# Layer norms whose sums lie in PSUM banks on VectorE and shift by the first tile; modulation tiles moved between up-projections

## The chip, the cores and the metric

The kernel runs on one core of one Trainium2 chip. A core has TensorE (PE in the profile; PEld is its weight load), VectorE (DVE), ScalarE (ACT), GpSimd (POOL) and SyncE (SP), each with its own queue of instructions, run in order. They tell each other of finished work through semaphores. SBUF and PSUM have 128 partitions; PSUM has eight banks of 512 fp32 columns. TensorE writes to PSUM alone, and GpSimd can't reach PSUM. The metric is the device time of one execution in microseconds (us).

## The reference

Four blocks follow each other on 512 tokens of width 1024 (blocks 2 and 3 also see 256 context tokens). Each block has a mixer (mLSTM, differential attention, convolution with a Fourier transform, neighbourhood attention) and a feed-forward part. Blocks 0 and 1 are built so:

```python
for i in range(2):
    ada = silu(c) @ w_ada[i] + b_ada[i]
    sh1, sc1, g1, sh2, sc2, g2 = split(ada, 6)
    u = x * (1 + sc1) + sh1
    y = mixer_i(u)
    x = layer_norm(ALPHA * x + (1 + g1) * y, ln_g[i, 0], ln_b[i, 0])
    u = x * (1 + sc2) + sh2
    h = causal_dwconv3(u @ w_up[i])            # 2 * 2816 channels
    a, g = split(h, 2)
    y = (gelu(g) * a) @ w_down[i]
    x = layer_norm(ALPHA * x + (1 + g2) * y, ln_g[i, 1], ln_b[i, 1])
```

Blocks 2 and 3 use RMS norms and a squared ReLU, with modulation vectors from `c_2` and `c_ctx_2`. All is fp32.

## The kernel before

**Layout.** Everything is feature-major: `XT` holds the residual stream as eight tiles of 128 features x 512 tokens. fp32 products are made of three matmuls with operands split into a high part (fp32r) and a low part: (WH, xh), (WH, xl), (WL, xh). A weight job is one output tile: SyncE loads 128 x 1024 fp32 into one of two `RAW` buffers (`load_raw`, L457), ScalarE rounds it into `WH` (`round_hi`, L788, or L857 in loops), GpSimd makes the low part `WL` (`lo`, L549), and TensorE runs 24 matmuls (L1503; L1177 in the value projection of block 1). `WH` and `WL` have four slots. `load_raw(j)` waits until the low part of job j-2 is made, and TensorE's job j waits for its own low part. Jobs are numbered through; the phases that matter here are the mixer's output projection `res`, and then for the feed-forward part three groups of an up-projection `up` (16, 16, 12 jobs) and a down-projection `down` (8 jobs each, the last with 18 matmuls a job). In block 0, `res` is jobs 32 to 39, the first `up` 40 to 55; in block 1 they are 132 to 139 and 140 to 155.

**Modulation.** The products with `w_ada` run on VectorE. SyncE loads a tile of 128 x 1024 (`load_ada`, L463, issued behind a weight load of the same queue), and VectorE multiplies it with the broadcast condition and sums (`ada_job`, L1630; two products, L1626 and L1627, for the tiles 96 to 159). A phase with `ada=a` does one tile per job, ahead of the job's own epilogue, from tile a on; `ada_out` writes four results into `MOD`. There are 192 tiles. The first up-projections carry 16 each, the third ones none.

**Up-projection epilogue.** ScalarE makes the first tap (L966), VectorE the two others out of the bank (`conv`, L1706), ScalarE the GELU, VectorE the product (`ffn_prod`, L638), ScalarE the high part (L634), VectorE the low part `Hl` (`ffn_lo`, L642). TensorE's down-projection waits for `Hl` tile by tile.

**Layer norms.** There are four, numbered by `idx` = 0 to 3, behind `res` and behind the last `down` of blocks 0 and 1. The variance is taken of shifted values. In the phase's first four jobs VectorE sums the finished tiles of `XT` into `ZS` (`sum_x`, L1714). TensorE multiplies the sum by 1/1024 into bank 5 (L1508), VectorE takes twice this mean of half the features off each tile (`shift`, L1729) and adds tiles 4 to 7 to `ZS` (L1734). ScalarE squares the tiles into `SQ` (L928). GpSimd adds squares 0 to 6 (`sum_squares`, L538), between the low parts of the next phase's first jobs. `ln_pe` sums over features with MEAN, token by token:

```python
pe.wait_ge(S("sq_add"), 6 * idx + 6)
token_sums(BANK[6], 0, SQ[:, 0], True, False)
pe.wait_ge(S("z_sum"), 2 * idx + 2)
token_sums(BANK[1], 0, ZS[:, 0:T], True, True).then_inc(S("d_sum"), 1)
pe.wait_ge(S("squared"), 8 * idx + 8)
token_sums(BANK[6], 0, SQ[:, 7], False, True).then_inc(S("var_sum"), 1)
```

A matmul with MEAN follows (L1542). `ln` on VectorE then centres (L1931) and scales (L1941) the tiles. ScalarE makes `U1h` and `UF`, and VectorE `U1l`. GpSimd's `norm_pool` (L511) applies gain and bias to `XT` as each `UF` tile is done, between its low parts of jobs 2 and 3 of the next phase. TensorE's first two jobs of that phase run side by side, tile by tile of `U1h` and `U1l`.

Of the kernel before, what the change touches and what calls it, by code (L numbers as in the profile page):

```python
# [54 lines left out]
LN_TILES = (((4, 0), (5, 1, 2), (6, 3), (7,)),) * 2 + (((), (4, 5, 0), (6, 1, 2, 3), (7,)), ((4, 0), (5, 1, 2), (6, 3), (7,)))  # L55
LN_HALF = (0, 0, 1, 0)

LN_MEAN = (3, 3, 3, 0)

NV_NORMS = ((0,), (1, 2), (3,), (4,), (5,), (6,), (7,), ())  # L60


def plan():
# [3 lines left out]
    def add(kind, n, layer, src, fill, nk=KT, ctx=False, ada=None, **more):  # L67
        nonlocal j0
        phases.append(dict(kind=kind, n=n, layer=layer, src=src, fill=fill, nk=nk, ctx=ctx, ada=ada,
                           j0=j0, seen=kinds.get(kind, 0), **more))  # L70
        j0 += n
        kinds[kind] = kinds.get(kind, 0) + n
        if ada is not None:
            assert ada == adas[-1]
            adas.append(ada + n)
# [16 lines left out]
    h = ffn(0, 8, 0, (40, 56, 64, 80, None, None))  # L92
# [4 lines left out]
    h = ffn(1, 24, h, (96, 112, 120, 136, None, None))  # L97
# [102 lines left out]
def build(nc, a, out):  # L200
    with ExitStack() as stack:
# [186 lines left out]

        def peeled(p):

            return p["j0"] == 0 or (p["seen"] == 0 and p["kind"] in ("v", "up", "na_k", "na_v", "res"))
# [59 lines left out]
        def _(sp):  # L451
# [28 lines left out]
            for n, p in enumerate(phases):  # L480
                def body(i, p=p, ada_before=None):
                    for u in range(4):
# [8 lines left out]
                if p["n"] > 4:  # L491
                    with sp.Fori(1, p["n"] // 4) as i:
                        body(i)
                pending = p["ada"] + p["n"] - 4 if p["ada"] is not None else None
# [8 lines left out]
        def norm_pool(pool, p):  # L503
            idx = 2 * p["layer"] + (p["kind"] == "down")
            for t in range(KT):
# [3 lines left out]
                else:  # L509
                    pool.wait_ge(S("uf_done"), 8 * UFILL[idx] + t + 1)  # L510
# [34 lines left out]
        def _(pool):  # L545
# [51 lines left out]
            for n, p in enumerate(phases):  # L597
# [23 lines left out]
                lo(p["j0"] + 3, 3, 1)  # L621
                if p["n"] > 4:
# [158 lines left out]
        def _(act):  # L781
# [138 lines left out]
            def shifted_squares(idx, u):  # L920

                if idx == 3 and u == 0:
# [3 lines left out]
                for n, t in ln_slots(idx, u):  # L926
# [3 lines left out]
            def epilogue(i, p, u):  # L930

                bank_out(i, p, u)
                if ends_in_ln(p) is not None and not is_first(i):
                    shifted_squares(ends_in_ln(p), u)
# [472 lines left out]
        def _(pe):  # L1407
# [72 lines left out]
            def stream(i, p):  # L1480
# [3 lines left out]
                for u in range(2 if after_norm else 0, 4):  # L1484
# [50 lines left out]
            def ln_pe(idx):  # L1535
                pe.wait_ge(S("sq_add"), 6 * idx + 6)
                token_sums(BANK[6], 0, SQ[:, 0], True, False)
# [3 lines left out]
                token_sums(BANK[6], 0, SQ[:, 7], False, True).then_inc(S("var_sum"), 1)  # L1541
                pe.matmul(BANK[LN_MEAN[idx]][:], MEAN[:], ZS[:, 0:T], start=True, stop=True).then_inc(S("mean_sum"), 1)  # L1542
# [67 lines left out]
        def _(dve):  # L1610
# [105 lines left out]
            def shift(i, p, u):  # L1716

                idx = ends_in_ln(p)
                if is_first(i):
                    sum_x(u)  # L1720
                    if u == 3:
                        dve.sem_inc(S("z_sum"), 1)
                    return
                if u == LN_HALF[idx]:
                    dve.wait_ge(S("mean_sum"), 2 * idx + 1)
                    link(dve.scalar_tensor_tensor(out=ZS[:, 0:T], in0=BANK[5][:], scalar=-8.0, in1=ZS[:, 0:T],
                                                  op0=ALU.mult, op1=ALU.add))
                for n, t in ln_slots(idx, u):
                    dve.scalar_tensor_tensor(out=XT[:, t], in0=BANK[5][:], scalar=-2.0, in1=XT[:, t], op0=ALU.mult, op1=ALU.add)\  # L1729
                        .then_inc(S("shifted"), 1)  # L1730
                for n, t in ln_slots(idx, u):
                    if t >= 4:
                        dve.wait_ge(S("shifted"), 8 * idx + n + 1)
                        link(dve.tensor_tensor(ZS[:, 0:T], ZS[:, 0:T], XT[:, t], ALU.add))  # L1734
# [179 lines left out]
            def ln(p, idx, nxt):  # L1914
# [12 lines left out]
                link(dve.tensor_tensor(SM[:, 48:52], BANK[6][:, 0:4], SM[:, 44:48], ALU.subtract))  # L1927
                dve.tensor_scalar(SM[:, 48:52], SM[:, 48:52], 0.0, None, ALU.max).then_inc(S("var_ready"), 1)

                def centre(t):  # L1930
                    dve.tensor_tensor(XT[:, t], XT[:, t], BANK[LN_MEAN[idx]][:], ALU.subtract).then_inc(S("centred"), 1)  # L1931
# [252 lines left out]
            for n, p in enumerate(phases):  # L2184
# [26 lines left out]
                def body(i, p=p):  # L2211
                    for u in range(4):
                        if p["ada"] is not None:
                            ada_job(i, p["ada"], u)
                        epilogue(i, p, u)
                    if p["ada"] is not None:
# [181 lines left out]
```

## Time and profile before

| | |
|---|---|
| median of 3 runs | 2957.94 us (2956.37 to 2958.21) |
| the profiled execution's own time | 2959.11 us |
| its span, from the first to the last instruction | 2957.3 us |
| mean granted TensorE clock | 0.972 |
| busy: PE, PEld | 2800.1 us (95%), 2392.5 us (81%) |
| busy: DVE, ACT, POOL | 1606.1 (54%), 1046.6 (35%), 1134.4 (38%) |
| chain that ended last, by engine | PE 81%, DVE 10%, issue 3%, POOL 3% |

Busy time is the union of an engine's instructions in the profile. The chain is followed back from the last instruction, at each step to what released it. A row of the timeline gives start, duration, engine (a q marks the queue's own work, such as issuing a DMA), line, operation, what it writes and reads, form, count, and in brackets the engine's idle time just before it with what ended it. The granted clock is given as a share of the upper of TensorE's two levels, 2.4 GHz; 0.50 is the lower one, 1.2 GHz. Matmuls are pipelined, so that a row's duration is longer than the distance to the next start.

### The profile page before, as it was taken

The page shows a single profiled execution, that of the slowest core. Times are in us where ns is not written, and L with a number is a line of the kernel's source. Part 1 is how long each engine was busy: PE and PEld are TensorE (multiplying, and loading weights), DVE is VectorE, ACT ScalarE, POOL GpSimd, SP SyncE. Part 2 cuts the span into 40 slices and gives each one's busy share as a digit, 9 for nine tenths or more (in the row PEclk, how much of TensorE's full clock was granted, in tenths as well). Part 3 has the DMA queues.
Part 4 walks back from the last instruction along what each step waited for, and adds up shares of the span by engine and source line. Part 5 has one row for each costly group of instructions (what it writes and reads, how often), then busy time and mean ns, then how long its engine had stood idle before and what let it go on. Part 6 is the DMA issues. An engine that isn't in the chain of part 4 may idle for free.

```text
span 2957.3 us, 38329 instructions
## 1 busy us (share of the span) xinstructions
PE 2800.1 (95%) x13904; PEld 2392.5 (81%) x13904; DVE 1606.1 (54%) x2329; ACT 1046.6 (35%) x1689; POOL 1134.4 (38%) x534
## 2 busy tenths in 40 slices
PE   4998899999999798999899999999999999999998
PEld 3885687887776687887897999999997977778887
DVE  6536885946455787976622332755453386432111
ACT  3333443423465443424321231212223337433222
POOL 2440554445522454445521243323235233334443
PEclk9998899999899899999799999999999999999999
DMA  5351355542421145543121122333332122122232
GB/s 214 109 185 43 114 195 188 185 149 93 144 83 61 57 176 181 197 149 114 45 64 59 56 74 76 138 119 129 127 128 78 53 95 65 61 82 97 93 99 85
DMA packets 89956, 329.84 MB, mean 112 GB/s; under 512 B 9956, under 2 KB 10724, under 8 KB 89320
## 3 DMA queue, kind: packets, MB, share of 16 engines
q1 hardware_dynamic: 85392, 312.21, 30.3%
q10 hardware_dynamic: 4440, 16.00, 1.6%
q8 instruction: 75, 1.23, 0.2%
q14 instruction: 49, 0.40, 0.0%
HBM read 324.50 MB, written 2.10 MB: 110 GB/s over the span
## 4 chain that ended last, share of the span: by engine, by line
PE 81%; DVE 10%; issue 3%; POOL 3%; ACT 2%; DMA 1%; DVEq 0%; ACTq 0%; SPq 0%; POOLq 0%
PE pair L1501 26%; PE pair L1503 26%; PE bank L1503 12%; PE pair L1192 3%; PE pair L1343 1%; DVE ADA L1630 1%; PE bank L1296 1%; PE pair L1359 1%; PE bank L1376 1%; DMA ADA<-in_ast 1%; DVE Hl L642 1%; DVE TA L638 1%; PE pair L1177 1%; PE bank L1177 1%; PE bank L1218 1%
## 5 line engine op out<-in xcount | busy, mean ns | idle before, releaser
L549 POOL TENSOR_TENSOR WL<-RAW,WH 128x1024 fp32r<-128x1024 f32 x392 | 977.4, 2495 | 1611.4 <-ACT WH L857 1089.3
L857 ACT ACTIVATE WH<-RAW 128x1024 fp32r<-128x1024 f32 x276 | 290.3, 1052 | 343.9 <-PE pair L1501 181.5
L1630 DVE CUSTOM_DVE_ANT_0 ADA<-ADA,CB 128x1024 f32<-128x1024 f32 x128 | 222.2, 1741 | 113.6 <-DMA ADA<-in_ast 102.5
L1750 DVE SCALAR_TENSOR_TENSOR XT<-pair,GATE,XT 128x512 f32 (+1 forms) x96 | 72.0, 751 | 346.4 <-PE pair L1503 180.5
L1501 PE MATMUL pair<-Uh,WH 128*128 128x384 f32 x832 | 214.1, 338 | 2.1 <-issue 1.6
L1501 PE MATMUL pair<-Uh,WL 128*128 128x384 f32 x832 | 211.1, 334 | 0.0
L1501 PE MATMUL pair<-Ul,WH 128*128 128x384 f32 x832 | 211.1, 334 | 0.0
L1503 PE MATMUL pair<-Hh,WH 128*128 128x512 f32 x432 | 173.2, 401 | 19.1 <-DVE Hl L642 19.1
L1503 PE MATMUL bank<-U1h,WH 128*128 128x512 f32 x480 | 187.3, 390 | 0.0
L1503 PE MATMUL bank<-U1h,WL 128*128 128x512 f32 x480 | 186.8, 389 | 0.0
L1503 PE MATMUL bank<-U1l,WH 128*128 128x512 f32 x480 | 186.7, 389 | 0.0
L1503 PE MATMUL pair<-U1h,WH 128*128 128x512 f32 x448 | 174.7, 390 | 0.0
L1503 PE MATMUL pair<-U1h,WL 128*128 128x512 f32 x448 | 174.4, 389 | 0.0
L1503 PE MATMUL pair<-U1l,WH 128*128 128x512 f32 x448 | 174.3, 389 | 0.0
L1503 PE MATMUL pair<-Hl,WH 128*128 128x512 f32 x432 | 171.0, 396 | 0.0
L1503 PE MATMUL pair<-Hh,WL 128*128 128x512 f32 x432 | 170.9, 396 | 0.0
L788 ACT ACTIVATE WH<-RAW 128x1024 fp32r<-128x1024 f32 x116 | 122.2, 1054 | 116.6 <-DMA RAW<-in_wst 54.4
L1501 PEld LDWEIGHTS pair<-Uh,WH 128*128 128x128 f32 x832 | 150.2, 188 | 6.1 <-issue 5.3
L1806 DVE SCALAR_TENSOR_TENSOR TT<-pair,TT 128x512 f32<-128x512 f32 x64 | 44.3, 692 | 197.3 <-ACT TT L978 103.5
L1501 PEld LDWEIGHTS pair<-Ul,WH 128*128 128x128 f32 x832 | 150.2, 188 | 0.0
L1501 PEld LDWEIGHTS pair<-Uh,WL 128*128 128x128 f32 x832 | 150.2, 188 | 0.0
L1501 PE MATMUL pair<-Hl,WH 128*128 128x384 f32 x512 | 129.9, 334 | 0.0
(408 smaller groups left out, 6244.6 us busy)
## 6 DMA issues: line engine op xcount, KB each, us to landing
RAW<-in_wst SPq DMA_DIRECT2D x392, 512.0 KB, 3.5
ADA<-in_ast SPq DMA_DIRECT2D x192, 512.0 KB, 4.5
NB<-in_nbias ACTq DMA_DIRECT2D x8, 768.0 KB, 4.2
XT<-in_xt SPq DMA_DIRECT2D x1, 2048.0 KB, 15.5
STRIP<-in_strip ACTq DMA_DIRECT2D x8, 256.0 KB, 2.8
CB<-in_cb ACTq DMA_DIRECT2D x4, 512.0 KB, 4.0
DX<-in_dx ACTq DMA_DIRECT2D x1, 2048.0 KB, 7.9
out_xt<-XT SPq DMA_DIRECT2D x1, 2048.0 KB, 6.2
```

The lines of the kernel that those rows point to most:

```text
L549: pool.tensor_tensor(WL[:, s4], RAW[:, s2], WH[:, s4].bitcast(F32), ALU.subtract)\
L638: dve.tensor_tensor(TA2[:, half], TA2[:, half], TG[:, half], ALU.mult).then_inc(S("ffn_prod"), 1)
L642: dve.tensor_tensor(flat(Hl[:, ds(tile, 1), 0:T]), TA2[:, half], flat(Hh[:, ds(tile, 1), 0:T]).bitcast(F32), ALU.subtract).then_inc(S("h_r ...
L788: act.activation(WH[:, u], RAW[:, u % 2], ACT.Copy).then_inc(S("hi_done"), 1)
L857: act.activation(WH[:, c % 4], RAW[:, c % 2], ACT.Copy).then_inc(S("hi_done"), 1)
L1177: mm = pe.matmul(BANK[VT_BANKS[half][b]][:], x[:, k, b * P:(b + 1) * P], flat(w[:, i, 4 * kk:4 * kk + 4]), start=k == 0 and m == 0, stop=k ...
L1192: mm = pe.matmul(BANK[j % 2][:], w[:, j % 4, k], x[:, k], start=k == 0 and m == 0, stop=k == KT - 1 and m == 2)
L1501: mm = pe.matmul(dst, w[:, u, k], x[:, k, c:c + HALF_TC], start=st and m == 0, stop=en and m == 2)
L1503: mm = pe.matmul(bank_of(p, u)[:], w[:, u, k], x[:, k, 0:T], start=st and m == 0, stop=en and m == 2)
L1630: dve.tensor_tensor_reduce(tile, tile, cb[:, 0], 1.0, 0.0, ALU.mult, ALU.add, AD[:, u, 0:1])\
L1750: ins = dve.scalar_tensor_tensor(out=flat(XT[:, ds(jl, 1)]), in0=bank[:], scalar=gate_of(jl), in1=flat(XT[:, ds(jl, 1)]), op0=ALU.mult, op ...
L1806: ins = dve.scalar_tensor_tensor(out=TT[:, u % 2, 0:T], in0=bank[:], scalar=0.0, in1=TT[:, u % 2, 0:T], op0=ALU.max, op1=ALU.mult)
```

## The change

**Sums and shift.** The shift is now eight times the feature mean of `XT[:, 0]` (`LN_SHIFT` names the job behind which TensorE makes it: 1, or 4 for norm 2). `LN_TILES` now gives for each of the eight jobs the tiles that are shifted in it. VectorE adds the shifted tiles in a PSUM bank (the last add writes `ZS`), and it also adds the squares 0 to 5 in another bank (`add_squares`; the last add writes `SQ[:, 0]`), a job later. Squares 6 and 7 are summed by TensorE as they are. GpSimd's `sum_squares` is gone. `LN_BANKS` names the banks. ScalarE loads the table of the square root in job 6 of the phase for norms 1 to 3.

**norm_pool.** For norms 0 to 2 it moves behind the low part of job 3 and waits for all eight `U1l` tiles instead of `UF` tile by tile.

**Modulation tiles.** The first up-projection of blocks 0 and 1 has them in its second half only (8 of 16 jobs). The phases after it carry on from there, and the last eight tiles are in the first eight of the third up-projection's 12 jobs. SyncE's and VectorE's loops of these four phases are written out.

```diff
-LN_TILES = (((4, 0), (5, 1, 2), (6, 3), (7,)),) * 2 + (((), (4, 5, 0), (6, 1, 2, 3), (7,)), ((4, 0), (5, 1, 2), (6, 3), (7,)))
-LN_HALF = (0, 0, 1, 0)
-
-LN_MEAN = (3, 3, 3, 0)
+LN_SHIFT = (1, 1, 4, 1)
+LN_TILES = (((), (0, 1), (2,), (3,), (4,), (5,), (6,), (7,)),) * 2 + \
+           (((), (), (), (), (0, 4, 1), (5, 2), (6, 3), (7,)), ((), (0, 1), (2,), (3,), (4,), (5,), (6,), (7,)))
+
+LN_BANKS = ((6, 3, 2, 3), (6, 3, 2, 3), (6, 7, 4, 3), (6, 3, 2, 0))
...
+ADA_GROUPS = {40: (2, 4), 80: (0, 2), 96: (2, 4), 136: (0, 2)}
...
-    h = ffn(0, 8, 0, (40, 56, 64, 80, None, None))
+    h = ffn(0, 8, 0, (40, 48, 56, 72, 80, None))
...
-    h = ffn(1, 24, h, (96, 112, 120, 136, None, None))
+    h = ffn(1, 24, h, (96, 104, 112, 128, 136, None))
...
+        def brings_ada(p, i):
+
+            return p["ada"] is not None and (p["ada"] not in ADA_GROUPS or p["groups"][0] <= i < p["groups"][1])
...
-                        elif not is_first(i) and p["ada"] is not None:
-                            load_ada(i * 4 + (p["ada"] - 4 + u), u % 2)
+                        elif not is_first(i) and brings_ada(p, i - 1):
+                            load_ada(i * 4 + (p["ada"] - 4 - 4 * p["groups"][0] + u), u % 2)
...
-                    pool.wait_ge(S("uf_done"), 8 * UFILL[idx] + t + 1)
+                    pool.wait_ge(S("u_ready"), 8 * UFILL[idx] + KT)
...
-        def sum_squares(pool, idx, n):
-
-            if n == 1:
-                pool.wait_ge(S("squared"), 8 * idx + 1)
-            else:
-                pool.wait_ge(S("sq_add"), 6 * idx + n - 1)
-            pool.wait_ge(S("squared"), 8 * idx + n + 1)
-            pool.tensor_tensor(SQ[:, 0], SQ[:, 0], SQ[:, n], ALU.add).then_inc(S("sq_add"), 1)
...
-                idx = ends_in_ln(before) if before is not None else None
                 for u in range(3):
                     lo(p["j0"] + u, u, u % 2)
-                    if idx is not None and u < 2:
-                        for n in ((1, 2, 3, 4), (5, 6))[u]:
-                            sum_squares(pool, idx, n)
-                if idx is not None:
+                idx = ends_in_ln(before) if before is not None else None
+                if idx == 3:
                     norm_pool(pool, before)
...
                 lo(p["j0"] + 3, 3, 1)
+                if idx is not None and idx != 3:
+                    norm_pool(pool, before)
...
+                if idx >= 1 and (i, u) == (1, 2):
+                    act.preload_act_table_set("sqrt_and_others")
...
-                    if idx is not None and not is_first(i) and u == LN_HALF[idx]:
+                    if idx is not None and 4 * i + u == LN_SHIFT[idx]:
                         pe.wait_ge(S("z_sum"), 2 * idx + 1)
-                        pe.matmul(BANK[5][:], MEAN[:], ZS[:, 0:T], start=True, stop=True).then_inc(S("mean_sum"), 1)
+                        pe.matmul(BANK[5][:], MEAN[:], XT[:, 0], start=True, stop=True).then_inc(S("mean_sum"), 1)
...
             def ln_pe(idx):
-                pe.wait_ge(S("sq_add"), 6 * idx + 6)
-                token_sums(BANK[6], 0, SQ[:, 0], True, False)
+                by_token, rest = (BANK[b] for b in LN_BANKS[idx][2:])
+                pe.wait_ge(S("sq_add"), 5 * idx + 5)
+                token_sums(by_token, 0, SQ[:, 0], True, False)
+                pe.wait_ge(S("squared"), 8 * idx + 7)
+                token_sums(by_token, 0, SQ[:, 6], False, False)
...
+                idx, jl = ends_in_ln(p), 4 * i + u
+                shifted, squares = (BANK[b] for b in LN_BANKS[idx][:2])
+                if jl == 0:
+                    dve.sem_inc(S("z_sum"), 1)
+                if jl == LN_SHIFT[idx]:
+                    dve.wait_ge(S("mean_sum"), 2 * idx + 1)
+                for n, t in ln_slots(idx, jl):
+                    dve.scalar_tensor_tensor(out=XT[:, t], in0=BANK[5][:], scalar=-8.0, in1=XT[:, t], op0=ALU.mult, op1=ALU.add)\
+                        .then_inc(S("shifted"), 1)
+                for n, t in ln_slots(idx, jl):
+                    dve.wait_ge(S("shifted"), 8 * idx + n + 1)
+                    if n:
+                        first_tile = XT[:, LN_TILES[idx][LN_SHIFT[idx]][0]]
+                        link(dve.tensor_tensor(ZS[:, 0:T] if n == 7 else shifted[:], first_tile if n == 1 else shifted[:], XT[:, t],
+                                               ALU.add))
+                if jl > LN_SHIFT[idx]:
+                    for n, t in ln_slots(idx, jl - 1):
+                        if not (idx == 2 and n == 5):
+                            add_squares(idx, n, squares)
+                if idx == 2 and jl == 6:
+                    add_squares(idx, 5, squares)
+
+            def add_squares(idx, n, squares):
+
+                if n == 0 or n > 5:
                     return
...
+                dve.wait_ge(S("squared"), 8 * idx + n + 1)
+                dve.tensor_tensor(SQ[:, 0] if n == 5 else squares[:], SQ[:, 0] if n == 1 else squares[:], SQ[:, n], ALU.add)\
+                    .then_inc(S("sq_add"), 1)
+                dve.wait_ge(S("sq_add"), 5 * idx + n)
...
-                        if p["ada"] is not None:
-                            ada_job(i, p["ada"], u)
+                        if brings_ada(p, i):
+                            ada_job(i - p["groups"][0], p["ada"], u)
...
-                if ends_in_ln(p) is not None:
-                    body(0)
-                    body(1)
+                if ends_in_ln(p) is not None or p["ada"] in ADA_GROUPS:
+                    for i in range(p["n"] // 4):
+                        body(i)
```

## Rows read from the trace of the kernel before

**Rows 1.** Who waited for whom (us in total, times, longest us), TensorE, whole span.
```profile
PE bank L1516 <- POOL SQ L538: 23.1, 4, 8.6
PE pair L1503 <- DVE Hl L642: 19.1, 11, 8.8
```

**Rows 2.** Timeline, the exit of norm 0.
```profile
340.93 0.43 SPq L463 DMA_DIRECT2D ADA<-in_ast  x1
...
345.76 1.23 DVE L1630 CUSTOM_DVE_ANT_0 ADA<-ADA,CB 128x1024 f32<-128x1024 f32 x1 [4.69 <-DMA ADA<-in_ast]
...
348.36 0.69 DVE L1734 TENSOR_TENSOR ZS<-ZS,XT 128x512 f32<-128x512 f32 x1
...
349.17 1.87 PE L1516 MATMUL pair<-MEAN,ZS 128*128 128x1 f32 x8 [3.71 <-DVEq L1916]
```

**Rows 3.** Timeline, the exit of norm 1.
```profile
734.63 1.23 DVE L1734 TENSOR_TENSOR ZS<-ZS,XT 128x512 f32<-128x512 f32 x1
...
740.12 1.85 PE L1516 MATMUL pair<-MEAN,ZS 128*128 128x1 f32 x8
```

**Rows 4.** The instructions of L1931 (duration ns min/median/max).
```profile
L1931 DVE TENSOR_TENSOR XT<-XT,pair x32: 673/680/689, 354.7 to 1424.6; 128x512 f32<-128x512 f32 x32
```

**Rows 5.** Timeline, the exit of norm 3.
```profile
1406.91 1.22 DVE L1734 TENSOR_TENSOR ZS<-ZS,XT 128x512 f32<-128x512 f32 x1
1408.28 3.67 DVE L1924 TENSOR_REDUCE CSQ<-UF 128x256 f32<-128x2048 f32 x1 [0.15 <-DVE ZS L1734]
...
1412.38 1.84 PE L1516 MATMUL pair<-MEAN,ZS 128*128 128x1 f32 x8
```

**Rows 6.** Timeline, the exit of norm 2.
```profile
1001.75 1.66 DVE L1740 SCALAR_TENSOR_TENSOR XT<-XT,TT 128x512 f32<-128x512 f32 x1
...
1015.32 1.84 PE L1516 MATMUL pair<-MEAN,ZS 128*128 128x1 f32 x8
```

**Rows 7.** Timeline of VectorE, job 1 of block 0's first up-projection.
```profile
380.15 3.44 DVE L1630 CUSTOM_DVE_ANT_0 ADA<-ADA,CB 128x1024 f32<-128x1024 f32 x1 [6.02 <-DMA ADA<-in_ast]
```

**Rows 8.** Waits of TensorE at 447-461, 585-592, 1112-1132 and 1255-1266.
```profile
PE pair L1503 <- DVE Hl L642: 3.4, 2, 2.2
...
PE pair L1503 <- DVE Hl L642: 0.9, 1, 0.9
...
PE pair L1503 <- DVE Hl L642: 9.3, 2, 8.8
...
PE pair L1503 <- DVE Hl L642: 1.7, 2, 1.2
```

**Rows 9.** Windows: length, busy us of PE, PEld, DVE, ACT, POOL, clock, DMA, GB/s.
```profile
372.00:448.00 76.00, 76.00 (x337) 62.90 (x337) 67.27 (x75) 33.70 (x44) 36.73 (x16) 1.00 0.56 201
...
457.00:461.00 4.00, 4.00 (x10) 3.07 (x10) 3.84 (x3) 1.64 (x2) 2.76 (x2) 0.50 0.14 47
...
1127.00:1132.00 5.00, 4.00 (x9) 2.70 (x10) 3.74 (x6) 2.54 (x4) 2.10 (x1) 0.50 0.02 5
```

**Rows 10.** Timeline: ScalarE's high part of job 3, TensorE's start of job 4, three phases.
```profile
370.31 1.05 ACT L788 ACTIVATE WH<-RAW 128x1024 fp32r<-128x1024 f32 x1
...
382.72 0.39 PE L1503 MATMUL pair<-U1h,WH 128*128 128x512 f32 x1
...
761.23 1.05 ACT L788 ACTIVATE WH<-RAW 128x1024 fp32r<-128x1024 f32 x1
...
775.29 0.39 PE L1177 MATMUL bank<-WH,U1h 128*128 128x512 f32 x1
...
1039.75 1.04 ACT L788 ACTIVATE WH<-RAW 128x1024 fp32r<-128x1024 f32 x1
...
1049.11 0.39 PE L1503 MATMUL pair<-U1h,WH 128*128 128x512 f32 x1
```

**Rows 11.** The instructions of L511 (duration ns min/median/max).
```profile
L511 POOL TENSOR_SCALAR XT<-XT,PRM x32: 772/1273/2327, 359.4 to 1430.1; 128x512 f32<-128x512 f32 x32
```

**Rows 12.** Groups of VectorE's instructions, 1037.8 to 1114.4 (busy us, mean ns, idle before).
```profile
L1706 DVE SCALAR_TENSOR_TENSOR TA<-pair,PRM,TA 128x511 f32<-128x511 f32 (+1 forms) x8 | 6.0, 747 | 0.5 <-DVE TA L1706 0.5
```

More of the change, by code:

```diff
@@ L68, in add @@
         nonlocal j0
-        phases.append(dict(kind=kind, n=n, layer=layer, src=src, fill=fill, nk=nk, ctx=ctx, ada=ada,
+        groups = ADA_GROUPS.get(ada, (0, n // 4))
+        phases.append(dict(kind=kind, n=n, layer=layer, src=src, fill=fill, nk=nk, ctx=ctx, ada=ada, groups=groups,
                            j0=j0, seen=kinds.get(kind, 0), **more))
@@ L74, in add @@
             assert ada == adas[-1]
-            adas.append(ada + n)
+            adas.append(ada + 4 * (groups[1] - groups[0]))
     add("qk", 16, 0, "u", 0)
@@ L487, in body @@
                             load_ada(ada_before + u, u % 2)
-                        elif not is_first(i) and p["ada"] is not None:
-                            load_ada(i * 4 + (p["ada"] - 4 + u), u % 2)
+                        elif not is_first(i) and brings_ada(p, i - 1):
+                            load_ada(i * 4 + (p["ada"] - 4 - 4 * p["groups"][0] + u), u % 2)
                 body(0, ada_before=pending)
-                if p["n"] > 4:
+                if p["ada"] in ADA_GROUPS:
+                    for i in range(1, p["n"] // 4):
+                        body(i)
+                elif p["n"] > 4:
                     with sp.Fori(1, p["n"] // 4) as i:
                         body(i)
-                pending = p["ada"] + p["n"] - 4 if p["ada"] is not None else None
+                pending = p["ada"] + 4 * (p["groups"][1] - p["groups"][0]) - 4 if brings_ada(p, p["n"] // 4 - 1) else None
             if pending is not None:
@@ L918, in rms_act, with shifted_squares @@
                     context_hi(KT - 1)
-            def shifted_squares(idx, u):
-                if idx == 3 and u == 0:
+            def shifted_squares(idx, i, u):
+                if idx >= 1 and (i, u) == (1, 2):
+                    act.preload_act_table_set("sqrt_and_others")
+                if idx == 3 and (i, u) == (1, 0):
                     act.wait_ge(S("ct_land"), 16)
@@ L925, in shifted_squares @@
                         act.activation(UF[:, t, T:TC], CT[:, t], ACT.Square).then_inc(S("ctx_sq"), 1)
-                for n, t in ln_slots(idx, u):
+                for n, t in ln_slots(idx, 4 * i + u):
                     act.wait_ge(S("shifted"), 8 * idx + n + 1)
@@ L932, in epilogue @@
                 bank_out(i, p, u)
-                if ends_in_ln(p) is not None and not is_first(i):
-                    shifted_squares(ends_in_ln(p), u)
+                if ends_in_ln(p) is not None:
+                    shifted_squares(ends_in_ln(p), i, u)
             def bank_out(i, p, u):
@@ L1540, in ln_pe @@
                 pe.wait_ge(S("squared"), 8 * idx + 8)
-                token_sums(BANK[6], 0, SQ[:, 7], False, True).then_inc(S("var_sum"), 1)
-                pe.matmul(BANK[LN_MEAN[idx]][:], MEAN[:], ZS[:, 0:T], start=True, stop=True).then_inc(S("mean_sum"), 1)
+                token_sums(by_token, 0, SQ[:, 7], False, True).then_inc(S("var_sum"), 1)
+                pe.matmul(rest[:], MEAN[:], ZS[:, 0:T], start=True, stop=True).then_inc(S("mean_sum"), 1)
                 if idx == 3:
@@ L1716, in shift @@
             def shift(i, p, u):
[L1718 to L1722, printed above, removed]
-                    return
[L1724 to L1734, printed above, removed]
+                idx, jl = ends_in_ln(p), 4 * i + u
```

10 lines of the change are left out of this document (6 added, 4 removed).

## Prediction, made before the change was run

> **What bounds the kernel now.** I read the page first: TensorE has work nearly throughout (the table above), so time can only be won where it stands or runs on a lower clock. The list of who waited for whom, cut to TensorE, names those places [rows 1]. Two of the groups lie where the change works. Four waits of 23.1 us together are for the sums of squares on GpSimd, one behind each layer norm. Eleven waits of 19.1 us together are for the low part of a hidden tile (`Hl`, L642), where a down-projection starts. I then read the timeline of each place. I call the norms N0 to N3 by `idx`, and give stretches in the profile's time.
>
> **The exits of the norms.** In the old code the last token sum over `ZS` may start only behind VectorE's last `ZS` add and behind the sum over `SQ[:, 0]`, which waits for GpSimd. What follows it (the sum over `SQ[:, 7]`, the mean matmul, centring) is the same in both kernels, so the start of the `ZS` sum measures each exit.
>
> N0: it starts at 349.17 [rows 2]. The last step's VectorE work is late because the modulation tile lands only at 345.7: it was issued at 340.93, behind a weight load that waits for GpSimd's low part, and that stood behind three sums of squares. Without those, low part 41 ends some 5 us earlier (about 335.7), its weight load and the modulation tile are issued at about 336.3, and the tile lands at about 341.0 by the same 4.7 us. Then come the tile product 1.2 (with up to 1 us of a lock), the residual 0.7, the shift 0.7 and the add 0.7: 345.3. Gain 3.9, with 3.0 and 5.5 as ends.
>
> N1: the last add starts at 734.63 and takes 1.23 because GpSimd runs; in a bank it takes the 0.68 of an operation that reads a bank and `XT` [rows 3, 4]. So 735.4 instead of 740.12: gain 4.7 (4.2 to 4.8). N3 is alike: 1406.91 + 0.68 and the hop give 1407.7 instead of 1412.38, gain 4.7 (4.0 to 4.8) [rows 5]. Here the context's `TENSOR_REDUCE` of 3.67 now starts at 1407.7 and ends at 1411.4, just when the last squares' sum does (1407.7 + 3.6). It costs nothing, but it would be what is late next.
>
> N2: VectorE has more to do, because shifts start only at job 4. From 1001.75 [rows 6] the step of tile 6 is residual 0.7, two shifts 1.4, two adds 1.3, three adds of squares 2.0 and a wait of 0.5 for ScalarE: 1007.7. The last tile needs 2.1 more: 1009.7 instead of 1015.32. Gain 5.6 (3 to 7).
>
> Together 18.9. VectorE's added work is three operations of 0.68 for each norm (20 instead of 17) and hides in the jobs: a step without a modulation tile is 2.8 us against jobs of 4.1 (18 matmuls of 0.226).
>
> The Trainium skill speaks against this ("VectorE: DVE Perf Modes", section "The TRN2 errata"): an operation that reads PSUM pays 120 fixed cycles where one from SBUF pays 58. By that page each exit would lose an estimated 0.065 us, 0.26 in all. The trace doesn't agree: 0.68 us with one operand in a bank [rows 4], 0.69 with both in SBUF at 348.36 [rows 2].
>
> **The first half of the first up-projection.** VectorE starts it late: at 380.15 it has waited 6.0 us for a modulation tile, whose product then takes 3.44, against 1.23 at 345.76 [rows 2, 7]. In block 1, where a tile costs two such products, it hardly catches up. The bill comes at the end of the phase, as `Hl` is late: 3.4 us of TensorE's wait in block 0 and 9.3 in block 1, where the second up-projections, also with a tile in each job but no norm ahead, pay 0.9 and 1.7 [rows 8]. Without tiles in the first eight jobs VectorE is freed of at least 8 x 1.2 us in block 0 and 16 x 1.2 in block 1, more than the lag. So the first up-projections should end like the second ones: 2.5 and 7.6 gained. Behind the longer waits TensorE's clock falls to the lower of its two levels (0.50 of the upper): from 457 to 461 it ran 10 matmuls, and in block 1 9 in 4.0 busy us, where 17.7 fit at the 0.226 us each of the phase's 76 us [rows 9]. That is 1.7 and 2.0 lost, and the slow clock lasts a little beyond both windows: I take 2.0 and 2.9. Together 4.5 + 10.5 = 15.0 (from 10.5, if block 0 ends no better than its third up-projection and block 1 keeps some lag, to 15.5).
>
> The eight tiles go to the third up-projection, jobs 0 to 7 of 12. Their DMAs go through SyncE's queue in the same pattern as in the second, where no weight came late. Four jobs without tiles follow, so its end stays. Cost 0; were that cover missing, up to the 10.5 of block 1. The loops written out in full I cost at 0.
>
> **norm_pool behind the low part of job 3.** This is the term against. The eight gain operations (L511) used to run between `U1l` tiles, mostly hidden. Now they stand between the low parts of jobs 3 and 4. ScalarE frees the high part of job 3 at the same point as before, so GpSimd ends low part 3 at about 373.8, 764.7 and 1043.3 (1.05 and 2.40 behind the starts of L788 at 370.31, 761.23 and 1039.75). TensorE wants low part 4 at 382.72, 775.29 and 1049.11 [rows 10]. In between must fit 8 d + 2.4, where d is the mean of L511: least 0.77, median 1.27, longest 2.33 [rows 11]. At 0.77 the stalls are 0, 0 and 2.8. At the median they are 3.7, 2.0 and 6.8: 12.5. I take 0.92: VectorE's operations there mostly read a bank (L1706, 0.747 on average with GpSimd at work [rows 12]), and only two `TA`/`Hl` operations can collide, 0.6 each. That gives 0.9, 0 and 4.0. The clock lost 2.0 behind a wait of 3.4, so I add that to the last: 6.9 in all. The ends are 2.8 and 19 (the median, with 2.0, 2.0 and 2.9 of clock). Queued behind it is also a weight load on SyncE, which waits for low part 4. It is due two jobs later (10.9 us), and landing 3.5, high part 1 and low part 2.4 fit.
>
> The Trainium skill has a rule for this ("SBUF — State Buffer", section "Who interferes with whom"): VectorE contends with GpSimd when both of its inputs are in SBUF, and the loser waits for the whole operation; with one input there is no contention. The trace agrees with the second half by the 0.747 of L1706. By that rule the stalls are the 4.9 us I took, by the median the 12.5.
>
> **Sum.** 18.9 + 15.0 - 6.9 = 27.0. The profiled execution took 2959.1 (its span is 2957.3); less 27.0 is 2932.1. The median of the runs shown is 2957.9, 1.2 lower, so I predict 2931.
>
> **Rivals.**
> 1. *As forecast*, 62%: 2931, own range 2925 to 2938.
> 2. *GpSimd's gain operations keep their old median*, 16%: 19 instead of 6.9, so 2943. For it: that is what they took. Against: then `U1l`, with both inputs in SBUF, ran beside them.
> 3. *Slower: the moved norm_pool starves TensorE*, 5%. At the longest duration, 2.33, the stalls are 12.1, 10.4 and 15.2 = 37.7, and each is followed by a slow clock as behind the 8.8 us wait, 2.9 each: 46.4, more than the 33.9 gained, so 2970. It decides from d = 1.8 (24 d - 18.1 + 8.7 = 33.9). Against it: only modulation products keep GpSimd off so long, and these have left that half.
> 4. *The tiles take their stall along* to the third up-projection, 7%: up to 10.5 back, 2941. For it: in block 1 a tile costs VectorE two products in each job. Against: four free jobs behind.
> 5. *The lag isn't from the tiles* but from the norm, so the ends of the first up-projections stay (the change does not do what it says), 6%: 15 less, 2946. Against: the 6.0 wait is for a tile.
> 6. Other, 4%.
>
> Cases 1, 2, 4 and most of 5 lie between 2923 and 2946, which leaves out the slower case and tails of the first, some 15 to 20%. A measurement of this kernel tells about 0.2% (6 us) from no change. Faster by more: 91%. Within: 4%. Slower: 5%.
>
> **What would show it.** No `SQ` on GpSimd, and TensorE's `ZS` sums some 4 to 5.6 us sooner behind the last job of each norm's phase. The waits for L642 at the first down-projections near 1 and 2 us. VectorE without a modulation product in the first eight jobs. L511 in one block behind low part 3 at 0.77 to 1 us each, and TensorE waiting for GpSimd's low part at job 4 of block 1, some 4 us. I am wrong if that wait is above 8, if waits for `Hl` come up in the third down-projection, or if the `ZS` sums move by under 3 us.

## The result, and the profile after

The changed kernel takes 2936.45 us (median of 4 runs, 2934.43 to 2938.15), the kernel before, on the same chip, 2958.07: ratio 0.9926, 95% interval 0.9913 to 0.9938. That is 21.6 us less, where 27 were forecast; 2931 was predicted, and 2936.45 lies within the range of 2923 to 2946. The profiled execution took 2937.88 us, with a span of 2936.1 against 2957.3. TensorE is busy for 2797.1 us, VectorE 1593.2, GpSimd 1093.2.

The waits of TensorE over the whole span, after (answers to [rows 1]; columns: us in total, times, longest):

```profile
PE pair L1507 <- DVE Hl L644: 8.1, 10, 1.2
...
PE bank L1520 <- DVE SQ L1752: 5.1, 1, 5.1
...
PE pair L1520 <- DVE SQ L1752: 4.3, 1, 4.3
```

The wait for hidden tiles fell from 19.1 to 8.1 us, and none is longer than 1.2. The 23.1 us for GpSimd's sums are gone. But two waits for sums of squares have come up on VectorE, 4.3 us in norm 0 and 5.1 in norm 2.

To find where time came from, I took the starts of TensorE's first and last matmul of each phase in both traces and set them against the terms of the prediction:

| stretch | before, us | after, us | gain | predicted |
|---|---|---|---|---|
| norm 0: last matmul of `res` to first of `up` | 19.35 | 20.04 | -0.7 | 3.9 |
| block 0, first up and down | 139.19 | 133.36 | 5.8 | 4.5 - 0.9 |
| block 0, third down | 37.41 | 35.57 | 1.8 | 0 |
| norm 1 | 18.63 | 13.55 | 5.1 | 4.7 |
| block 1, value projection, to the first scores | 61.19 | 64.90 | -3.7 | 0 |
| norm 2 | 20.28 | 18.47 | 1.8 | 5.6 |
| block 1, first up | 89.32 | 93.58 | -4.3 | -6.0 |
| block 1, first down | 56.29 | 45.50 | 10.8 | 10.5 |
| norm 3 | 32.12 | 27.37 | 4.7 | 4.7 |

These make 21.3 us; the span lost 21.2. The row of the value projection runs on through two and a half jobs of the next projection, up to the first matmul of the attention scores; all of its 3.7 us were lost in the value projection itself. Norms 1 and 3 and the down-projections came out near what was worked out, and the first up-projection of block 1 lost less. Norms 0 and 2 gave 1.1 of the 9.5 us predicted for them, and the value projection lost 3.7 that weren't foreseen.

**Norm 0.** Timeline after, one turn of what sets its pace and the end (answers to [rows 2]):

```profile
337.05 0.63 ACT L932 ACTIVATE SQ<-XT 128x512 f32<-128x512 f32 x1 [4.35 <-DVE XT L1732]
337.59 1.04 ACT L790 ACTIVATE WH<-RAW 128x1024 fp32r<-128x1024 f32 x1
...
338.71 2.39 POOL L552 TENSOR_TENSOR WL<-RAW,WH 128x1024 fp32r<-128x1024 f32 x1 [4.11 <-ACT WH L790]
...
341.13 0.33 SPq L467 DMA_DIRECT2D RAW<-in_wst  x1
341.50 0.43 SPq L473 DMA_DIRECT2D ADA<-in_ast  x1
...
346.14 2.49 DVE L1637 CUSTOM_DVE_ANT_0 ADA<-ADA,CB 128x1024 f32<-128x1024 f32 x1 [1.16 <-DMA ADA<-in_ast]
...
348.56 0.68 DVE L1760 SCALAR_TENSOR_TENSOR XT<-XT,TT 128x512 f32<-128x512 f32 x1
349.28 0.69 DVE L1732 SCALAR_TENSOR_TENSOR XT<-bank,XT 128x512 f32<-128x512 f32 x1
350.00 0.69 DVE L1738 TENSOR_TENSOR ZS<-bank,XT 128x512 f32<-128x512 f32 x1
350.00 0.63 ACT L932 ACTIVATE SQ<-XT 128x512 f32<-128x512 f32 x1 [4.30 <-DVE XT L1732]
```

Read it from square to square. ScalarE's square at 337.05 had waited 4.35 us for VectorE's shift; the high part queued behind it, then GpSimd's low part, the weight load, the modulation tile behind that on SyncE (341.50; 340.93 before), its product on VectorE, residual, shift, and the square at 350.00. That is 12.95 us for two jobs of 5.44. The work goes around a ring: each part waits for the one before it, and the last one feeds the first again, two jobs later, at 6.5 us a job. The product of 2.49 is part of it, 1.23 without a wait: it started beside a low part (345.20 to 347.55). Without those 1.26 us a turn would be 5.85 us a job, an estimate from these rows, still more than 5.44. In the kernel before, ScalarE did that high part 6.1 us ahead of the phase's last matmul (339.42), here 2.8 us ahead (340.38), and GpSimd's sums delayed only the low part behind it:

```profile
332.39 5.34 POOL L538 TENSOR_TENSOR SQ<-SQ 128x512 f32<-128x512 f32 x3 [0.38 <-ACT SQ L928]
...
333.35 1.04 ACT L788 ACTIVATE WH<-RAW 128x1024 fp32r<-128x1024 f32 x1
...
337.69 2.83 POOL L549 TENSOR_TENSOR WL<-RAW,WH 128x1024 fp32r<-128x1024 f32 x1
```

**Norms 1 and 3.** The `ZS` sums, after (answers to [rows 3] and [rows 5]): 2.8 us behind each phase's last matmul, 7.5 before. Before, the last add had ended at 735.86 in norm 1, and TensorE waited for GpSimd's sums up to 740.12; that wait was 4.3 us. The context's reduction of 3.63 starts right behind the add and ends 0.2 us behind the last squares' sum, as foreseen.

```profile
729.39 1.46 PE L1520 MATMUL pair<-MEAN,ZS 128*128 128x1 f32 x8 [0.75 <-DVEq L1936]
...
1391.93 1.78 PE L1520 MATMUL pair<-MEAN,ZS 128*128 128x1 f32 x8 [0.75 <-DVEq L1936]
1391.98 3.63 DVE L1944 TENSOR_REDUCE CSQ<-UF 128x256 f32<-128x2048 f32 x1 [0.16 <-DVE ZS L1738]
```

**Norm 2.** Timeline after (answers to [rows 6]):

```profile
988.66 0.67 ACT L992 ACTIVATE TT<-pair,GATE 128x512 f32<-128x512 f32 x1
988.84 2.39 POOL L552 TENSOR_TENSOR WL<-RAW,WH 128x1024 fp32r<-128x1024 f32 x1 [4.16 <-ACT WH L790]
989.43 2.34 DVE L1760 SCALAR_TENSOR_TENSOR XT<-XT,TT 128x512 f32<-128x512 f32 x1 [0.95 <-ACT TT L992]
...
1002.13 0.69 DVE L1752 TENSOR_TENSOR SQ<-bank,SQ 128x512 f32<-128x512 f32 x1
1002.86 1.02 DVE L1760 SCALAR_TENSOR_TENSOR XT<-XT,TT 128x512 f32<-128x512 f32 x1
...
1002.88 3.54 PE L1520 MATMUL bank<-MEAN,SQ 128*128 128x1 f32 x16 [5.11 <-DVE SQ L1752]
1006.28 1.84 PE L1520 MATMUL pair<-MEAN,ZS 128*128 128x1 f32 x8
```

The residual (`XT` and `TT`, both in SBUF) takes 2.34 us where 0.7 was put in: GpSimd's low part began 0.59 us ahead of it, and it ended 0.5 us behind that low part. The `ZS` sum starts 8.9 us behind the phase's last matmul (997.38), 10.7 before, 5.1 predicted. VectorE's last add had ended at 1005.32; the sum stood 0.9 us longer behind the 16 matmuls over the squares, which waited for the add at 1002.13.

**norm_pool.** GpSimd's eight gain operations, and TensorE at job 4 of block 1's up-projection:

```profile
754.12 6.06 POOL L524 TENSOR_SCALAR XT<-XT,PRM 128x512 f32<-128x512 f32 x8
...
1034.04 6.06 POOL L524 TENSOR_SCALAR XT<-XT,PRM 128x512 f32<-128x512 f32 x8
...
1042.65 0.47 PE L1507 MATMUL pair<-U1h,WH 128*128 128x512 f32 x1 [2.79 <-POOL WL L552]
```

They take 0.76 us each, where 0.92 was taken; the stall of 2.8 is what was worked out for 0.77. In the 5 us behind it the granted clock is 0.66. The windows from 1043 to 1048 and of the rest of the phase (columns as in [rows 9]):

```profile
1043.00:1048.00 5.00, 5.00 (x17) 3.91 (x16) 2.60 (x2) 2.05 (x3) 2.68 (x2) 0.66 0.61 210
...
1048.00:1109.00 61.00, 61.00 (x271) 50.51 (x270) 48.00 (x65) 26.06 (x35) 31.78 (x13) 1.00 0.48 172
```

The value projection, jobs 4 to 6 of GpSimd and SyncE:

```profile
760.14 4.75 POOL L552 TENSOR_TENSOR WL<-RAW,WH 128x1024 fp32r<-128x1024 f32 x2
762.57 0.33 SPq L467 DMA_DIRECT2D RAW<-in_wst  x1
...
766.03 1.06 ACT L790 ACTIVATE WH<-RAW 128x1024 fp32r<-128x1024 f32 x1 [6.14 <-DMA RAW<-in_wst]
766.99 1.07 ACT L963 ACTIVATE VD<-pair 128x512 f32<-128x512 f32 x2
...
767.62 0.80 PE L1181 MATMUL pair<-WH,U1h 128*128 128x512 f32 x1 [2.52 <-ACT VD L963]
```

TensorE doesn't wait for a low part here. It waits for ScalarE's copies out of its banks, which stand behind a high part, whose weight load waited for low part 4, which waited for norm_pool.

### The profile page after: what moved, and what is told of

The parts are those of the page before. It is cut to its first block, busy times and chain, and to the rows that moved or that the text cites. A ratio compares the mean times of both kernels' runs of the same rounds, so it can differ in the third digit from the quotient of the medians.

```text
span 2936.1 us, 37960 instructions
## 1 busy us (share of the span) xinstructions
PE 2797.1 (95%) x13936; PEld 2391.5 (81%) x13936; DVE 1593.2 (54%) x2341; ACT 1046.6 (36%) x1689; POOL 1093.2 (37%) x510
## 3 DMA queue, kind: packets, MB, share of 16 engines
q8 instruction: 75, 1.23, 0.2%
## 4 chain that ended last, share of the span: by engine, by line
PE 58%; DVE 2%; POOL 1%; ACT 1%; issue 1%; DVEq 0%; ACTq 0%; POOLq 0%
PE pair L1505 26%; PE pair L1507 18%; PE bank L1507 4%; PE pair L1347 1%; PE bank L1300 1%; PE pair L1363 1%; PE bank L1380 1%; PE bank L1347 1%; PE bank L1437 0%; PE pair L1461 0%; PE pair L1320 0%; PE bank L1320 0%; POOL UF L534 0%; PE bank L1287 0%; POOL UF L538 0%
## 5 line engine op out<-in xcount | busy, mean ns | idle before, releaser
L1637 DVE CUSTOM_DVE_ANT_0 ADA<-ADA,CB 128x1024 f32<-128x1024 f32 x128 | 237.7, 1863 | 117.2 <-DMA ADA<-in_ast 105.9
L1505 PE MATMUL pair<-Hh,WL 128*128 128x384 f32 x512 | 129.9, 334 | 0.0
```

Of the source, the lines that this page charges most:

```text
L1505: mm = pe.matmul(dst, w[:, u, k], x[:, k, c:c + HALF_TC], start=st and m == 0, stop=en and m == 2)
L1637: dve.tensor_tensor_reduce(tile, tile, cb[:, 0], 1.0, 0.0, ALU.mult, ALU.add, AD[:, u, 0:1])\
```

## The experiments

Each kernel was timed beside the kernel before (2958.7 to 2959.8 us in these runs). Intervals are 95%. A norm's time is counted from TensorE's last matmul of the projection to its first of the next phase, as in the table.

**tiles_only.** The kernel before with the modulation tiles' part of the diff alone (`ADA_GROUPS`, the list of the phases' tiles, the loops written out).

> The kernel before with the modulation tiles moved and nothing else; the norms and norm_pool are the old ones. Theory 1 (the parts add up): in the changed kernel's trace the first up- and down-projections gained 5.8 us in block 0 and 10.8 in the down-projection of block 1, and the last up-projections of block 0 1.8 more; all of it comes from the tiles, so this kernel gains 16 to 18.5 of the 21.6 us: 2940 to 2942, with waits of about 1 us for the low part of the hidden tile at both first down-projections. Theory 2 (part of the lag came from the old norms, whose last additions start VectorE late into the up-projection): it gains under 13, above 2945, and a wait of over 3 us for the hidden tile stays in one of the blocks.

Measured: 2945.74 us (2945.26 to 2948.99, 5 runs), ratio 0.9958 [0.9944, 0.9971]: 12.9 gained. Both first down-projections wait 1.2 us at most at a time; block 0's first down takes 44.27 us, its third 35.61, block 1's first down 45.47: 18.3 gained there, as theory 1 has it. But 5.8 us are lost in block 1's attention, where nothing was edited. Its trace there:

```profile
875.97 2.34 POOL L558 TENSOR_TENSOR WL<-RAW,WH 128x1024 fp32r<-128x1024 f32 x1 [7.18 <-ACT WH L797]
876.00 2.72 DVE L2102 SCALAR_TENSOR_TENSOR PD<-ZD,SM,PD 128x384 f32<-128x384 f32 x1
...
878.78 0.90 PE L1237 MATMUL bank<-IDENT,PD 128*128 128x128 f32 x3 [2.27 <-DVE PD L2102]
```
```profile
870.00:885.00 15.00, 12.48 (x51) 9.07 (x49) 9.27 (x24) 6.32 (x21) 2.34 (x1) 0.77 0.20 69
```

VectorE's operation began 0.03 us behind GpSimd's low part and took 2.72 us; in the changed kernel the same one (876.42, 0.62 us) missed it. TensorE waited 2.3, and over these 15 us its clock was 0.77, against 1.00 before. So neither theory's total fits: the tiles gave all of the 18.3, and an accident of phase took 5.8 back. That it is an accident is argued, not shown: it was not tried by itself. No other kernel here shows it.

**tiles_unmoved.** The other half: the changed kernel with `ADA_GROUPS = {}` and the old list of tiles.

> The changed kernel with the modulation tiles where they were: only the norms and norm_pool's place are changed. Theory 1 (the parts are not independent: norm_pool's eight gain operations now meet a modulation product of VectorE in each job, and each such product or gain operation waits for the other): the 18.3 us of the tiles are lost, and the gain operations take 1.2 us or more each instead of 0.76, so that TensorE waits some 4 us more in each of the three phases: 2958 to 2968, no faster than the kernel before. Theory 2 (the parts add up, gain operations stay at 0.76): 2936.5 + 18.3 = 2954.8.

Measured: 2962.46 us (2958.03 to 2967.46, 11 runs), ratio 1.0012 [1.0003, 1.0021]: slightly slower than before. (The profiled execution took 2967.45, the second longest of the eleven.) GpSimd's eight gain operations now take 7.02 us in block 0 and 9.03 in block 1, and TensorE waits twice as long at job 4 there:

```profile
1048.55 9.03 POOL L524 TENSOR_SCALAR XT<-XT,PRM 128x512 f32<-128x512 f32 x8
```
```profile
PE pair L1507 <- POOL WL L552: 5.7, 1, 5.7
```

The first down-projections lose more than the tiles had cost: 52.53 and 55.03 us, 17.8 more than in the changed kernel, where moving the tiles had gained 16.5. The parts depend on each other, as in theory 1, though its 1.2 us for each gain operation was too much (0.88 and 1.13).

**pool_old_place.** norm_pool back, the rest as changed:

```diff
-                    pool.wait_ge(S("u_ready"), 8 * UFILL[idx] + KT)
+                    pool.wait_ge(S("uf_done"), 8 * UFILL[idx] + t + 1)
-                if idx == 3:
+                if idx is not None:
                     norm_pool(pool, before)
                 lo(p["j0"] + 3, 3, 1)
-                if idx is not None and idx != 3:
-                    norm_pool(pool, before)
```

> The changed kernel with norm_pool for norms 0 to 2 back between the low parts of jobs 2 and 3, tile by tile behind UF. Theory 1 (the move costs what TensorE's segments lost: 3.7 us in block 1's value projection, 4.3 in its first up-projection): 8 us faster than the changed kernel, about 2928.5, and no wait of TensorE for the low part of a weight near 765 us, none of 3 us at job 4 of the up-projection. Theory 2 (GpSimd's gain operations only shift which low part is late; in the old place low part 3 is, and more of them meet operations of VectorE with two operands in SBUF): 2934 to 2938, with waits at job 3. Theory 3: the 3.7 us in the value projection come from the new sums around norm 1 and not from norm_pool, so only about 4 come back: 2932.

Measured: 2929.31 us (2925.86 to 2930.95), ratio 0.9897 [0.9882, 0.9912], 7.1 below the changed kernel. The value projection takes 60.86 us and block 1's first up 89.59: 4.0 each, theory 1. A gain operation's median there is 1.27 us again, and costs nothing: it stands in work that waits for ScalarE anyway. Its trace also has norm 1 at 11.66 us against 13.55, and the next kernel's at 11.39, where nothing was edited: in the 3 us behind the `ZS` sum the granted clock was 0.90 here (731 to 734) and 0.58 in the changed kernel (729.4 to 732.4). A difference of 2 us in one stretch can be the clock alone.

**vt_copies_first.** In the value projection's fourth job:

```diff
                     for u in range(4):
-                        round_next(i, p, u)
+                        late = p["kind"] == "vt" and is_first(i) and u == 3
+                        if not late:
+                            round_next(i, p, u)
                         epilogue(i, p, u)
+                        if late:
+                            round_next(i, p, u)
```

> The changed kernel with one thing swapped: in the fourth job of block 1's value projection ScalarE copies the four banks out (VD) first and only then makes the high part of the weight three jobs on. Theory 1 (TensorE's wait of 2.52 us at 767.62 is for those copies, which stand behind a high part whose weight load is late: it waits for low part 4, that for norm_pool): the wait goes, block 1's value projection takes about 61.5 instead of 64.90 us, and the time is 3 to 3.5 less, about 2933. Theory 2 (behind the copies TensorE would wait for the low parts themselves, which are as late): the wait moves to the low part of weight 5 or 6 and less than 1 us comes back, 2936.

Measured: 2932.81 us (2929.98 to 2936.83), ratio 0.9916 [0.9902, 0.9929]; the value projection 61.09. Copies at 762.56, no wait behind them, though norm_pool is still where the change put it: theory 1.

```profile
762.56 1.09 ACT L963 ACTIVATE VD<-pair 128x512 f32<-128x512 f32 x2 [5.44 <-PE bank L1185]
```

**squares_later.** ScalarE squares the tiles of a job behind the next high part:

```diff
+                if ends_in_ln(p) is not None and 4 * i + u > 0:
+                    shifted_squares(ends_in_ln(p), *divmod(4 * i + u - 1, 4))
                 bank_out(i, p, u)
-                if ends_in_ln(p) is not None:
+                if ends_in_ln(p) is not None and (i, u) == (1, 3):
                     shifted_squares(ends_in_ln(p), i, u)
```

> The changed kernel with ScalarE's square of each shifted tile one job later, behind the high part of the next weight instead of ahead of it. Theory 1 (norm 0 is late through a ring: the square waits for VectorE's shift and holds up the high part, that the low part, the weight load, the modulation tile behind it in SyncE's queue, and that VectorE's next step; 6.5 us a turn against 5.44 us of a job): the modulation products of the last steps start at TensorE's pace, TensorE's sum over ZS in norm 0 starts 3 to 5 us sooner, the other norms change by less than 1, and the time is 2931.5 to 2933.5. Theory 2 (norm 0 is late because VectorE and GpSimd lock each other out in each step, which the order on ScalarE doesn't touch): the sum over ZS moves by less than 1 us and the time stays at 2935.5 to 2937.5.

Measured: 2931.41 us (2929.69 to 2933.06), ratio 0.9905 [0.9889, 0.992]. Norm 0 fell from 20.04 to 12.67 us: the ring was open, the last tile was issued at 334.62 and the `ZS` sum stands 3.4 us behind the last matmul (340.57), where the changed kernel had 10.4.

```profile
334.62 0.43 SPq L473 DMA_DIRECT2D ADA<-in_ast  x1
...
339.41 1.35 DVE L1639 CUSTOM_DVE_ANT_0 ADA<-ADA,CB 128x1024 f32<-128x1024 f32 x1 [0.26 <-DMA ADA<-in_ast]
...
343.98 1.52 PE L1522 MATMUL pair<-MEAN,ZS 128*128 128x1 f32 x8 [1.35 <-DVEq L1938]
```

With the order went also most of the wait in the product, 1.35 instead of 2.49 us; how much of the 7.4 us is the order alone and how much that wait was not taken apart. The other norms changed little, but norm 2 lost 1.1 (19.56).

**both** and **two_edits.** Both edits; then the same with norm 2 keeping its order (`later = idx in (0, 1, 3)`).

> Both edits together: norm_pool in its old place and ScalarE's squares one job later. Theory 1 of both: the gains add, as they lie in other stretches (norm 0's phase; the jobs behind norms 1 and 2): 2936.5 - 8 - 4 = 2924.5. If only the order on ScalarE matters, 2932; if only norm_pool's place, 2928.5.

> norm_pool in its old place, and ScalarE's squares one job later for norms 0, 1 and 3 alone; norm 2 keeps its order. Theory 1 (with the later squares norm 2 took 19.55 us from the last matmul of its projection to the first of the up-projection, against 18.47 with the early ones, since the order on ScalarE isn't what holds it): norm 2 is back at 18.5 and the time is 1 us below the kernel with both edits, 2923.5. Theory 2 (the 1.1 us are chance): 2924.5 as there.

Measured: 2924.74 us (2923.98 to 2926.0), ratio 0.9883 [0.9868, 0.9898], the sum of the two; and 2921.89 (2920.25 to 2927.04), ratio 0.9879 [0.9864, 0.9894], with norm 2 at 18.43. Their intervals overlap, so the 1.1 us of norm 2 rest on the traces: 19.6 in both kernels with the later squares there, 18.3 to 18.5 in the five that change nothing there against the changed kernel.

**short_low.** The changed kernel, with GpSimd's low parts around norm 2 made for one slice of eight (`WL[:, s4, 0:1]` and the like for `D_RES + 3 <= j <= D_RES + 10`); it leaves seven eighths of them out.

> The changed kernel, with GpSimd's low part of eight weights (jobs 3 to 7 of block 1's mixer output projection and jobs 0 to 2 of the up-projection behind it) made for one of their eight slices of input features only; seven eighths of these low parts are left out. Theory 1 (around norm 2 each residual of VectorE, with both operands in SBUF, waits for GpSimd's low part of the same step: 2.0 to 2.5 us instead of 0.7): the residuals take 0.7, VectorE's steps are some 1.6 us shorter, and TensorE's sum over ZS starts 2.5 to 4.5 us sooner behind the projection's last matmul than the 8.9 us of the changed kernel, about where the prediction had it (5.1). Theory 2 (VectorE only waits for ScalarE there, and the locks fill waits that stay): the sum over ZS moves by less than 1 us.

Measured: 2929.23 us (2926.93 to 2931.02, 4 runs), ratio 0.9893 [0.9877, 0.991]. Every residual takes 0.69 us, VectorE's steps follow each other at TensorE's pace, and norm 2 takes 13.07 instead of 18.47. The `ZS` sum starts 3.6 us behind the last matmul, 5.3 sooner; theory 1 gave 2.5 to 4.5.

```profile
986.70 0.69 DVE L1764 SCALAR_TENSOR_TENSOR XT<-XT,TT 128x512 f32<-128x512 f32 x1 [1.37 <-ACT TT L996]
...
999.97 1.74 PE L1524 MATMUL pair<-MEAN,ZS 128*128 128x1 f32 x8 [0.29 <-DVEq L1940]
```

**n2_sums_on_pe.** Two edits, and `SQ_ADDS = (5, 5, 2, 5)`: for norm 2 TensorE sums the squares 3 to 6.

> The kernel with the two edits, and for norm 2 VectorE adds only the squares 0 to 2; TensorE, which stands idle there for 5 us behind its last job, sums squares 3 to 6 over the features itself, ahead of the sum over ZS. Theory 1 (VectorE sets norm 2's exit: three additions of squares, 2.1 us, stand ahead of its last residual, and 16 matmuls of 3.4 us wait for the last of them): the sums end 1 to 1.5 us sooner, norm 2 takes about 17.2 us, the time is 2922.3. Theory 2 (seven sums of 1.7 us are as long as what they replace): no change within 0.5 us.

Measured: 2923.56 us (2920.22 to 2926.17), ratio 0.9881 [0.9866, 0.9896]. Norm 2 took 17.62, 0.8 less, but block 1's third down 1.6 more, with no edit there. That lies between the theories, and no gain can be measured.

**n2_out_first** and **n0_n2_out_first.** Two edits, and around norm 2 (then norm 0 as well) ScalarE's high part moved behind the taking out of the bank. Around norm 0 the square of the tile before already stood between the two, so there the high part comes behind both:

```diff
-                round_next(i, p, u)
                 bank_out(i, p, u)
+                round_next(i, p, u)
```

> The kernel with the two edits, and around norm 2 ScalarE takes the bank out (TT, what VectorE's residual reads) before it makes the next high part, instead of behind it. Theory 1 (the lock comes from their order: the high part ends first, so GpSimd's low part starts ahead of VectorE's residual and holds it for 1.6 us in each step; with the bank out first the residual is done before the low part begins): residuals of 0.7 us, norm 2 from 18.4 to 14 or 15 us, 2918 to 2919. Theory 2 (the lock moves to the first additions with both operands in SBUF, or the later high parts make the low parts late): under 1 us of change, or TensorE waits for a low part.

> The same order around norm 0 as well. Theory 1 (there the lock falls on the modulation product ahead of the residual, 2.49 instead of 1.22 us, and a later high part also makes weight load and modulation tile later): norm 0 gains nothing or loses 1 to 3 us against the kernel with norm 2 alone. Theory 2 (the residual is freed as in norm 2): norm 0 gains 1 us or more.

Measured: 2918.42 us (2914.89 to 2919.24), ratio 0.9857 [0.9841, 0.9874], the fastest of all, 18 us below the changed kernel. Norm 2 takes 13.20, 5.2 less than with two edits; block 1's second down, with no edit and the same waits, took 1.6 more. The residual is through before the low part begins:

```profile
983.26 1.05 ACT L788 ACTIVATE WH<-RAW 128x1024 fp32r<-128x1024 f32 x1
983.47 0.69 DVE L1763 SCALAR_TENSOR_TENSOR XT<-XT,TT 128x512 f32<-128x512 f32 x1 [0.62 <-ACT TT L996]
...
984.39 2.41 POOL L552 TENSOR_TENSOR WL<-RAW,WH 128x1024 fp32r<-128x1024 f32 x1 [3.03 <-ACT WH L788]
```

With norm 0 as well it is 2933.22 us (2931.85 to 2934.17), ratio 0.991 [0.9893, 0.9927]. Norm 0 takes 26.47 us, 13.5 more than with its own order. The direction is theory 1's, its 1 to 3 us far too little: the high part stands behind a square that waits for VectorE again, so the ring closes. With the bank's copy in it too, and with 1.8 us of waiting in each product (3.03 for 1.23), it turns at 7.0 us a job, product to product.

```profile
344.87 3.03 DVE L1640 CUSTOM_DVE_ANT_0 ADA<-ADA,CB 128x1024 f32<-128x1024 f32 x1 [1.18 <-DMA ADA<-in_ast]
...
351.91 3.01 DVE L1640 CUSTOM_DVE_ANT_0 ADA<-ADA,CB 128x1024 f32<-128x1024 f32 x1 [1.22 <-DMA ADA<-in_ast]
```

## Why the prediction was right, and where its steps were not

- **N1 and N3, 4.7 each: right.** The `ZS` sums came 4.7 us sooner: 4.3 of wait for GpSimd's sums, and the last add, 0.69 instead of 1.23. That this add escapes GpSimd because it reads a bank isn't shown there, since the low part had just ended (728.53, the add began at 728.59). It is in norm 2: the add of squares at 1002.13 took 0.69 beside a low part that ran from 1000.98 to 1003.33.
- **N0, 3.9: wrong, -0.7.** The step that failed is "low part 41 ends some 5 us earlier". I took what GpSimd stopped doing and left its input where it was. Even with its input in place the step was too early: the high part ended at 334.39, so a low part of 2.4 can't end before 336.8, where 335.7 was written. And that input, ScalarE's high part, went from 333.35 to 337.59. Squares that wait for VectorE stood ahead of the last three high parts before, too (326.76, 333.35, 340.17, so 6.6 and 6.8 apart); the change spreads the shifts over the jobs, so they stand ahead of six, from 311.63 on, and the lag adds up over twice as many turns. The wait moved from GpSimd to ScalarE. With that order undone, norm 0 gave 6.7 us against before (squares_later, 12.67 against 19.35).
- **N2, 5.6: mis-sized, 1.8.** VectorE's count of operations was right; "residual 0.7" was not, at 2.0 to 2.5 beside GpSimd's low part. The prediction's own row of before showed a longer residual there (1.66 at 1001.75 [rows 6]). The sum also left out that the `ZS` sum stands behind TensorE's sum of the squares, 0.9 us in the trace. The Trainium skill ("SBUF — State Buffer", section "Who interferes with whom") says that VectorE and GpSimd contend when both VectorE inputs lie in SBUF. The prediction used that rule for norm_pool and not here. The runs agree with it: 2.34 us beside a low part, 0.69 without (short_low) or ahead of it (n2_out_first).
- **First up-projections, 15.0: right in mechanism, a little too small.** The down-projections gave 5.7 and 10.8, where 4.5 and 10.5 were taken and 15.5 was the upper end for both. Their own price of 0 for the third up-projection stands (rival 4 is out), rival 5 too: tiles_only gives the same without the new norms. Not foreseen were 1.8 us of the third down in block 0, where the waits stayed (1.9 and 1.7 us) and the granted clock went from 0.96 to 1.00. They came with the moved tiles in every kernel (37.4 with the old places, 35.6 with the new), but what lifts the clock is open.
- **norm_pool, 6.9: 8.0, in other places.** Nothing in block 0 (0.9 predicted), 4.3 in block 1's up (6.0 predicted, 2.8 + 2.0 at the d of 0.76 that was measured), and 3.7 in the value projection, priced at 0. There the failed step is "landing 3.5, high part 1 and low part 2.4 fit": the low part would have fitted, but the high part stood ahead of ScalarE's copies, which are due at once (vt_copies_first). Rivals 2 and 3 are out: d was 0.76. It stays low because the tiles left that half: with them back (tiles_unmoved) it is 0.88 and 1.13, on the way to rival 2's 1.27 and far from rival 3's 1.8.

So that the total came near was in part luck, as errors of both signs met: 8.4 us too much in norms 0 and 2 and 3.7 in the value projection, against 1.8 of clock, 4.2 too little in the first up- and down-projections and 0.4 in norm 1.

## What to carry to other kernels

When work is taken off one engine, ask when the input of what was behind it is made: follow the chain back over all the queues until it meets the same tile again, and if its turn is longer than a job, the ring is the bound and not the work taken away. A wait for a neighbouring engine belongs behind what others need from the same queue: here the order of two or three of ScalarE's instructions was worth 7.4 us (norm 0), 5.2 (norm 2) and 3.8 (the value projection). And the right order differs by place: the high part as the later one gains 5 us in norm 2, where no modulation tile hangs on it, and costs 13 in norm 0, where one does and a square stands ahead.

## What the runs showed of the hardware

- VectorE's operation with both operands in SBUF that starts 0.03 to 0.6 us behind a GpSimd operation of 2.4 us ends 0.4 to 0.5 us behind that one's end (2.72 instead of 0.62 in tiles_only, 2.34 instead of 0.69 in the changed kernel). An add with one operand in a bank took 0.69 beside such an operation (1002.13). Such a meeting moves with edits upstream: one went with 5.8 us in a part of the kernel that wasn't touched, 2.3 as a wait and the rest mostly by the granted clock of 0.77.
- A modulation product waits in turn: 6.00 us in the changed kernel (at 759.98), where two low parts on end ran from 760.14 to 764.89, and 5.37 in vt_copies_first, against 1.22 alone.
- The granted clock differs where the waits do not: a down-projection with the same two waits, 1.7 us in all, took 45.58 us in two_edits and 47.19 in n2_out_first.
